# Earlier release of the softmax outputs' PSUM bank, a second row buffer, and another placing of convolution taps and pooling steps

## The reference, cut to what matters

```python
# first block: four mixers on h = adaptive_norm(x), each 4 heads x 64
y_a = nsa_attention(...)            # compressed + selected + window attention, gated
y_b = banded_attention(..., SWA_WINDOW, slopes, sink)
y_c = stick_breaking_attention(...)
y_d = retention(...)
for i, (y, z) in enumerate(branches):
    yi = y * silu(z)
    merged += sigmoid(h @ w_merge[i]) * (yi @ w_br[i])
x = rms_norm(x + gate * (merged @ w_out), final_g)
# second block
z = rms_norm_2(h, g) @ w_in
y_conf = conformer_conv(conf_ab, ...)      # a * sigmoid(b), causal depthwise conv of 31 taps, layer norm, silu, matmul
y_att  = forgetting_attention(q, k, v, f)  # softmax with a cumulated forget row, causal
y_sc   = short_conv_mixer(...)
y_pool = multiscale_pool(pool_v, ...)      # causal means over 2, 4, 8, 16 tokens minus the value, then a matmul
h = h + rms_norm_2(concat(...) @ w_out, g)
h = h + rms_norm_2(square(relu(norm(h) @ w_up)) @ w_down, g)
h = h + rms_norm_2((p @ w_ple_proj) * sigmoid(norm(h) @ w_ple_gate), g)
```

## Time and profile before

| | |
|---|---|
| median of 3 runs | 2757.73 us |
| profiled execution | 2758.56 us |
| its span, first to last instruction | 2756.8 us |
| mean granted PE clock | 0.957 of full |
| chain that ended last, share of PE | 85% |
| the same, DVE / issue / ACT / POOL | 6% / 3% / 3% / 2% |
| HBM read and written | 123.97 and 8.39 MB |

### The profile page before, as it was taken

One profiled execution on the slowest core, in us unless ns is written; L12 is line 12 of the kernel. 1 busy time (PEld: TensorE's weight loads), 2 busy tenths in 40 slices (PEclk: granted clock), 3 DMA queues, 4 the chain that ended last, 5 costly groups with the idle time before them and its releaser, 6 DMA issues.

```text
span 2756.8 us, 30013 instructions
## 1 busy us (share of the span) xinstructions
PE 2559.4 (93%) x12580; PEld 1987.4 (72%) x12580; DVE 929.0 (34%) x1175; ACT 828.9 (30%) x1219; POOL 864.6 (31%) x424
## 2 busy tenths in 40 slices
PE   7999999898998888999999989889999999999896
PEld 4777778555686665687876656678888888888785
DVE  6314320444304455202158563314022222222423
ACT  4104541454423554312223433233211111111421
POOL 2112212434323111244532210345223333233633
PEclk8999999999998999999999998999999999999898
DMA  7101011100020000012121000210111111111111
GB/s 294 46 24 46 30 33 48 35 13 27 23 81 29 11 20 9 27 51 99 46 100 39 24 24 22 92 46 24 54 46 54 46 46 46 54 46 46 52 39 71
DMA packets 34582, 135.35 MB, mean 49 GB/s; under 512 B 3664, under 2 KB 4112, under 8 KB 33040
## 3 DMA queue, kind: packets, MB, share of 16 engines
q1 hardware_dynamic: 34128, 132.38, 13.8%
q10 hardware_dynamic: 320, 1.05, 0.1%
HBM read 123.97 MB, written 8.39 MB: 48 GB/s over the span
## 4 chain that ended last, share of the span: by engine, by line
PE 85%; DVE 6%; issue 3%; ACT 3%; POOL 2%; DMA 0%; POOLq 0%; SPq 0%; DVEq 0%; ACTq 0%
PE slot L727 57%; PE slot L773 13%; PE ps L958 2%; PE ps L934 2%; PE ps L805 2%; PE ps L919 1%; PE ps L944 1%; POOL wlo L1597 1%; PE ps L1001 1%; PE ps L848 1%; PE ps L989 1%; PE ps L831 1%; PE ps L1020 1%; DVE ada_sum L2138 0%; PE ps L889 0%
## 5 line engine op out<-in xcount | busy, mean ns | idle before, releaser
L727 PE MATMUL slot<-xhi,whi 128*128 128x512 f32 x2192 | 722.9, 412 | 43.6 <-DVE xlo L2287 14.7
L1597 POOL TENSOR_TENSOR wlo<-raw,whi 128x1024 fp32r<-128x1024 f32 (+1 forms) x169 | 429.9, 2544 | 888.7 <-ACT whi L1210 888.7
L727 PE MATMUL slot<-xlo,whi 128*128 128x512 f32 x2192 | 695.4, 399 | 0.0
L727 PE MATMUL slot<-xhi,wlo 128*128 128x512 f32 x2192 | 691.9, 397 | 0.0
L727 PEld LDWEIGHTS slot<-xhi,whi 128*128 128x128 f32 x2192 | 408.1, 194 | 163.4 <-issue 83.1
L727 PEld LDWEIGHTS slot<-xlo,whi 128*128 128x128 f32 x2192 | 424.2, 194 | 93.5
L727 PEld LDWEIGHTS slot<-xhi,wlo 128*128 128x128 f32 x2192 | 422.3, 193 | 92.9
L1210 ACT ACTIVATE whi<-raw 128x1024 fp32r<-128x1024 f32 (+1 forms) x169 | 186.3, 1102 | 357.5 <-PE slot L773 174.7
L773 PE MATMUL slot<-uhi,whi 128*128 128x512 f32 x512 | 158.3, 390 | 0.0
L1388 ACT ACTIVATE ptr<-ps 128x256 f32<-128x256 f32 (+3 forms) x176 | 80.0, 454 | 260.7 <-PE ps L934 260.3
L773 PE MATMUL slot<-ulo,whi 128*128 128x512 f32 x512 | 157.7, 389 | 0.0
(11 more groups left out here) (330 smaller groups left out, 2802.1 us busy)
## 6 DMA issues: line engine op xcount, KB each, us to landing
raw<-wstream SPq DMA_DIRECT2D x129, 512.0 KB, 3.2
raw<-wstream SPq DMA_DIRECT2D x40, 640.0 KB, 3.9
ada<-wada SPq DMA_DIRECT2D x7, 1024.0 KB, 20.0
mm<-xT SPq DMA_DIRECT2D x2, 2048.0 KB, 9.8
ada<-wada SPq DMA_DIRECT2D x2, 2048.0 KB, 27.0
mm<-xT SPq DMA_DIRECT2D x8, 512.0 KB, 4.6
res_dram<-mm SPq DMA_DIRECT2D x8, 512.0 KB, 3.0
res<-res_dram SPq DMA_DIRECT2D x8, 512.0 KB, 6.5
```

The costliest lines, as they stand in the source:

```text
L727: o = mm_(outs[:, half * HALF:(half + 1) * HALF], w[b % 2][:, k_w, :], x[:, k_x, half * HALF:(half + 1) * HALF], start=first and j == 0, s ...
L1597: tt(flat(wlo[b % 2])[:, 0:n], (raw1 if b == 1 else raw)[:, 0:n], flat(whi[b % 2])[:, 0:n].bitcast(F32), ALU.subtract).then_inc(w_lo, 1)
```

## The change

It has three parts. In SEL and WIN the product in `outputs` counts up a semaphore of its own, `s_taken`, and the factor rows of pairs 17 to 48 wait for it instead of for the end of `outputs`; the addition L1990 waits for it too, in place of the chain semaphore. `frow` becomes two tiles, used in turn, and ACT's copy of pair p waits for the output of pair p-2. In the FGT stage the taps and pooling steps are no longer spread evenly: they go only in front of a dense part that directly follows a `bias`, `factor` or `values` step (one or two in each such place), the taps alone up to block Ep1, then alternating with the pooling.

```diff
+def placed(events, *groups):
+
+    at = {}
+    for places, steps in zip(groups[::2], groups[1::2]):
+        for k, step in enumerate(steps):
+            at.setdefault(places[k * len(places) // len(steps)], []).append(step)
+    return [e for i, ev in enumerate(events) for e in at.get(i, []) + [ev]]
...
-    rest = spread(proj[soft:], steps)
+    rest = [ev for ev in spread(proj[soft:], steps) if ev[0] != "gap"]
     pooled = rest.index(("dense", INDEX["Ep1"], PARTS["F"] - 1)) + 1
     late = conv[NTAPS_EARLY:]
-    ahead = len(late) * pooled // len(rest)
     pool = [("pool", 0, 4), ("pool", 0, 5)] + [("pool", 1, step) for step in range(6)]
+    quiet = [i for i in range(1, len(rest)) if rest[i][0] == "dense" and rest[i - 1][0] in ("bias", "factor", "values")]
+    early = sum(i <= pooled for i in quiet)
+    ahead = (len(late) + len(pool)) * early // len(quiet)
     behind = [ev for pair_ in itertools.zip_longest(pool, late[ahead:]) for ev in pair_ if ev]
+    rest = placed(rest, quiet[:early], late[:ahead], quiet[early:], behind)
...
-    tl += spread(rest[:pooled], late[:ahead]) + spread(rest[pooled:], behind)
+    tl += rest
...
-        frow = at("frow", small_at[0], [P, P])
+        frow = [at("frow0", small_at[0], [P, P]), at("frow1", 185, [P, P])]
...
             def factor_rows(p):
                 pe.wait_ge(s_fac, p + 1)
-                pe.wait_ge(s_norm, p)
+                if U_SEL < p <= U_FGT:
+                    pe.wait_ge(s_taken, p - U_SEL)
+                elif p:
+                    pe.wait_ge(s_norm, p)
...
                     act.wait_ge(s_row, ev[1] + 1)
-                    nc.scalar.activation(frow[:], ps7[:, P:2 * P], ACT.Copy).then_inc(s_rowsb, 1)
+                    if ev[1] >= 2:
+                        act.wait_ge(s_norm, ev[1] - 1)
+                    nc.scalar.activation(frow[ev[1] % 2][:], ps7[:, P:2 * P], ACT.Copy).then_inc(s_rowsb, 1)
...
-                y = yfm[:, t, i * P:(i + 1) * P]
+                y, f = yfm[:, t, i * P:(i + 1) * P], frow[p % 2][:]
...
                 if ph in ("SEL", "WIN"):
-                    link(v.tensor_tensor(frow[:], ps7[:, 0:P], frow[:], ALU.mult))
-                    v.tensor_tensor(y, frow[:], y, ALU.add).then_inc(s_norm, 1)
+                    v.tensor_tensor(f, ps7[:, 0:P], f, ALU.mult).then_inc(s_taken, 1)
+                    dve.wait_ge(s_taken, p - U_SEL + 1)
+                    v.tensor_tensor(y, f, y, ALU.add).then_inc(s_norm, 1)
                 else:
-                    v.tensor_tensor(y, ps7[:, 0:P], frow[:], ALU.mult).then_inc(s_norm, 1)
+                    v.tensor_tensor(y, ps7[:, 0:P], f, ALU.mult).then_inc(s_norm, 1)
```

More of the change, by code:

```diff
@@ L554, in build @@
             sem(n) for n in ("k_z", "k_abs", "k_log", "k_sp", "k_sum", "k_r", "k_a", "k_mask", "k_o", "k_y"))
-        k_hi, k_lo, k_neg, dist_in = sem("k_hi"), sem("k_lo"), sem("k_neg"), sem("dist_in")
+        k_hi, k_lo, k_neg, dist_in, s_taken = (sem(n) for n in ("k_hi", "k_lo", "k_neg", "dist_in", "s_taken"))
         c_pos, c_h, c_hs, c_kv, c_kvs, c_s, c_sb, c_e, c_p, c_t, c_tb, c_o, c_y = (
```

## The result

The change makes the kernel a little slower: 2762.72 us median of 22 runs (21 of them at 2759.98 to 2765.52, one at 2749.94) against 2757.03 for 22 runs of the kernel before beside it, ratio 1.0016, 95% interval [1.001, 1.0023]; by the medians 5.7 us. Forecast were 2749.7 us and a range of 2744 to 2756. The profiled execution took 2763.97 us, span 2762.2, mean granted clock 0.954 (before 0.957).

What follows compares the result with a forecast made beforehand. TensorE, busy 93%, was taken to bound the kernel. Bank -5.35, places 0.0 and clock -2.7 summed to -8.0 us, 2749.7 us for the median from 2757.73; range 2744 to 2756.

Steps and rivals of the forecast that it cites:

- The bank: Factor rows of pairs 17 to 48 wait for the product alone, not the addition: minus 5.35 us of PE's waits.
- The long place: Wait near 1097 us, where the addition lasts 2.34 us beside POOL: PE would start 2.38 us earlier.
- The clock at 1098 us: Half-speed stretch behind the wait at 1097 us would not come once that wait shrinks: minus 2.7 us.
- The places: Six changed places of taps and pooling in DVE's forget-stage order: sum 0.0 us, bounds minus 5 and plus 2.2.
- Pair 48: First factor of the forget stage: two taps now stand ahead of it, so PE waits, plus 3.35 us.
- Pair 57: Its output in the forget stage: the tap ahead of it is gone, minus 1.3 us.
- rival 3: Forget stage slower: DVE overruns where two steps now stand, 1.29 us each on PE; 2765.3 us, chance 0.05.
- pair 62: Its scores in the forget stage: a pooling step moves behind, minus 2.7 us, or 0.5 gained if POOL is first.
- The clock of the forget stage: Low-clock stretches behind forget-stage waits: net 0, ends plus 1.7 us (one more) and minus 3.4 (two fewer).
- Rival 1: The clock gives nothing, its fall near 1097 us coming anyway; 2752.4 to 2754.1 us, taken as 2753.3, chance 0.22.
- Rival 4: Early release ends only the long place's wait, 2.4 us, and POOL is first at pair 62; 2757.5 us, chance 0.06.
- rival 2: Forget stage also speeds up, low-clock stretches at pairs 57 and 62 going: 3.4 us more, 2746.3 us, chance 0.22.

Runs made afterwards that it cites:

- e9: e4 with one row buffer instead of two, ACT's copy waiting for the addition of the pair before; 2740.11 us, ratio 0.9934.
- e5: Kernel before with only taps 0 and 1 of tile 1 put ahead of pair 48's factor; 2762.59 us, ratio 1.0018.
- e3: Kernel after with taps 0 and 1 of tile 1 moved from ahead of pair 48's factor to behind pair 50's bias; 2752.0 us, ratio 0.998.
- e2: Kernel before with the new order of taps and pooling steps alone, no early release; 2764.91 us, ratio 1.0026.
- e1: Kernel after with the order of taps and pooling steps of before, so the early release alone; 2755.87 us, ratio 0.9991.
- e10: Early release limited to factor rows of pairs 17 to 43, with the order of taps and pooling of before; 2748.76 us, ratio 0.9967.
- e13: e4 with the early release limited to pairs 17 to 43; 2738.71 us, ratio 0.9929.
- e4: Kernel after, but with the tap order of before and seven taps and pooling steps moved behind operations PE waits for; 2739.84 us, ratio 0.9933.
- e11: e4 with the early release limited to pairs 17 to 32; 2738.8 us, ratio 0.9932.

## Why the prediction was wrong

By its steps:

- **The bank, -5.35 us: right.** PE's idle time in the attention stretch fell by 4.7 us, the waits named in the rows by 5.0. The long place gave what was worked out (0.85 us left of 3.22). The small loss against 5.35 is a second and third factor wait (4.8 us in two became 5.6 in three), of the kind foreseen once. The second row buffer, for which the sum has no term, gave 0.6 at most (e9).
- **The clock at 1098 us, -2.7 us: right in its stretch**, 221.17 to 218.45 us of busy time, and the low stretch at 1098 us is gone. That the figure is met so closely is in part luck: of the other low stretches there, two became 3.4 us longer, one 3.4 shorter, and one of 3.4 went, which cancels. (The low stretch of before began 1.35 us ahead of the wait's end, 1099.65 less 1098.30, and not 1.2 as the prediction's first rival has it; nothing hangs on it.) That the gain stays won was never asked. The between stretch, which the prediction did not look at and so put at nothing, lost 4.0 us, 3.7 of them busy time; this term failed too. The loss is there in every one of the six kernels with the release of all pairs (377.6 us each), and in none of the seven traces with no release or one up to pair 41 (373.4 to 373.6). After the change there is a low stretch of 3.4 us at 1124.1 us that before had not, and the norm's sums at 1370 us have 13.7 us of low clock for 10.2.
- **The places, 0.0 us: the waits were nearly right.** Pair 48: +3.35 forecast, 3.23 seen. Pair 55: 2.88 to 4.6, forecast 4.5. Pair 57: 1.88 to 0.59, forecast 0.6. Pair 51: 1.39 to 0.56 at factor rows 50. No wait of 1.3 us came where two steps now stand, so rival 3 did not happen. The exception is pair 62: forecast -2.7, and the scores' wait went from 4.10 to 3.34, that at the factor rows behind them from 1.72 to 1.06, 1.4 in all. At pair 61's output 0.3 us went where none was forecast. The six places sum to +1.1 us of waits. The lines there:

```profile
1650.80 4.79 DVE L1850 SCALAR_TENSOR_TENSOR scy<-zs,vec,scy 128x1023 f32<-128x1023 f32 x2
...
1652.16 2.35 POOL L1614 TENSOR_TENSOR wlo<-raw,whi 128x1024 fp32r<-128x1024 f32 x1 [14.36 <-ACT whi L1225]
...
1656.56 0.78 PE L931 MATMUL ps<-khif,qpf 64*128 64x512 f32 x2 [3.34 <-DVE ring L1959]
```

  Esc0's last tap is the one that POOL's split holds: 3.47 us instead of 1.25. That is the case for which the prediction gave 0.5 in place of 2.7. The recorded starts would not have told it: the tap began at 1652.12, 0.04 us ahead of POOL, and was held all the same. The rule that the prediction quoted from the Trainium skill ("SBUF — State Buffer", the shared port pair: whichever starts first gets it) would, by these starts, have held POOL here. Recorded starts 0.04 us apart may not tell which was first, so this trace neither bears the rule out nor refutes it.
- **The clock of the forget stage, taken as 0 with +1.7 and -3.4 as ends: this step failed.** It was +6.0 us, of a loss of 7.0. The prediction did see that the new wait at pair 48 "should bring one" low stretch, and priced it at 1.7 us. It brought two: 6.8 us right behind it, and 10.2 us at pair 56's bias rows, in dense work; one of 3.4 us (at 1627 us) went with pair 57's wait. That is 13.6 us more of low clock, which costs up to half its length where it is full of matmuls: 6.8 us, and 6.0 by the busy time. e5 shows that these two taps alone bring a loss of that size, e3 that taking them away repairs it.
- **How the wait brings the low clock at pair 56 is not shown.** In every trace all low stretches begin and end on one regular beat, and a longer wait at pair 48 also moves the rows of pair 56 on that beat. Read from the clock changes in the fifteen traces, the first of those rows begins 0.8 to 1.2 us behind the beat in the three kernels with low clock there (after, e2, e5) and 1.4 to 3.2 us behind it in the twelve without. So the wait may have cost its 10.2 us of low clock only because it moved the rows to a bad place, and another shift of the work might do the same without a wait. No run moved them without changing the wait.

The sum with the measured terms: -4.7 - 2.7 + 3.7 + 0.3 (between) + 1.0 + 6.0 = +3.6 us, and the timed difference is +5.7. The 2 us between the two are of the size that one execution's start-up or clock differs from the next (2.5 us between these two traces). Against the forecast of -8.0 that is 13.7 us: 6.0 the clock of the forget stretch, 4.0 the between stretch, 1.0 the places, 0.7 the bank, and those 2.

Rival 1, that the clock gives nothing, was right for the bank as a whole, though by another way than it said: the low stretch at 1098 us did go. By time e1 is 1.9 us faster than before, where 8.0 were expected of the bank. Rival 4 is out (the waits fell by 5.0), and so is rival 2 (the forget stretch became 7.0 us longer).

**The between stretch, 373.5 or 377.6 us.** It follows the program where the release is total (six of six) or ends by pair 41 or is left out (all seven), and for the release up to pair 43 it went once each way with identical work. What separates all fifteen traces is again the place on the beat: the stretch begins 0.2 to 0.7 us behind the beat in the seven traces with 377.6 or 377.9 us, and 1.0 to 1.4 us behind it in the eight with 373.4 to 373.7. In e10 (0.2) and e13 (1.0) the work was already 0.5 us apart on the beat when the attention stretch began, before any of it differed. Five of the six with 377.6 begin the attention stretch at the same place, 1.8 to 1.9 us behind the beat, although their start-ups took 248.0 to 250.9 us, and run it in 244.4 or 244.5 us, so they reach the between stretch at the same place too.

The Trainium skill ("TensorE: Matmul & The Clock Gate", on the clock gate) says that the monitor behind the clock is free-running, that it does not start with the kernel; that agrees with 373.7 and 377.9 us for one order, and with the one execution of the kernel after at 2749.94 us among 21 at 2760 and more. **What stays open** is whether the place on the beat is the cause, since no run moved the work by itself, and why most executions come to the same place. It also doesn't tell e9 and e13 (182.2 and 182.3 us in the forget stretch) from e4 and e11 (179.2 and 179.3): all four begin that stretch 2.6 to 2.8 us behind the beat. Many profiled executions of one program would settle it; they were not taken.

## What to carry to other kernels

A new wait on a tensor engine that is 93% busy can cost its length and clock besides, here 3.2 us and another 4 to 7, some of it 64 us later in work that waits for nobody. A wait of 1.95 us at the same place cost 3.4 in all, so this is no fixed price. Compare busy time at equal instruction counts between fixed marks, not only waits, and carry that comparison past the stage that was changed. A rule for where filler goes ("only where dense parts begin") is worth less than a look at each wait: seven steps moved behind the operation that PE was waiting for gave 16 us, the steps placed by the rule lost 7. An experiment should have each part alone, since here a gain of 2 us was hidden under a loss of 7.

## What the runs showed of the hardware

- The granted clock fell to 0.50 for 10.2 us while PE was busy for all of them (after, e2 and e5, each at pair 56's bias rows with their matmuls on 4 partitions), and did not in the same work of the kernels with a wait of 1.95 us or none at pair 48. The three also have these rows at one place on the beat of the clock's changes (0.8 to 1.2 us behind it); the runs can't part the two.
- Loss out of proportion to the wait: one of 3.23 us at pair 48 against 1.95 costs 5.8 us of PE's busy time, 1.95 against none 1.6 (181.20, 175.42, 173.87 us).
- A low stretch taken away can come back in the next stage: both kernels have 54.6 us of low clock from the attention stretch to the first forget scores, 27.3 + 27.3 before and 20.5 + 34.1 after. It need not: e13 has 20.5 + 27.3.
- The same work in the same order took 373.7 us in one trace and 377.9 in another (e13, e10), and in all fifteen traces the longer time goes with a begin 0.2 to 0.7 us behind the beat on which the granted clock changes, the shorter with one 1.0 to 1.4 us behind it.
- A two-input VectorE operation that began 0.04 us ahead of a GpSimd one, by the record, was the one held: 3.47 us instead of 1.25.
